# A hybrid decoder layer on one core: new start addresses for the operands of the down products

## The chip, the cores and the metric

The kernel runs on one core of a Trainium2 chip. The metric is the device time of one execution in microseconds (us); smaller is better. TensorE multiplies, VectorE (DVE), ScalarE (ACT) and GpSimd (POOL) do the elementwise work, SyncE (SP) issues most transfers.

## What is computed

One layer over 1056 tokens (1024 of a prompt and 8 x 4 of running sequences), width 1024, all in float32:

```
x = x + 0.5 * rmsnorm(swiglu_ffn(rmsnorm(x, g1), w_gu1, w_down1), p1)      # D_FF = 2816
x = x + rmsnorm(concat(conv_module(u), rg_lru(u)) @ w_out, pm)             # u = rmsnorm(x) @ w_in
x = x + 0.5 * rmsnorm(swiglu_ffn(rmsnorm(x, g2), w_gu2, w_down2), p2)
x = x + rmsnorm(sigmoid(rmsnorm(x) @ w_gate) * (p @ w_proj), pp)

def swiglu_ffn(x, w_gu, w_down):
    gate, up = jnp.split(x @ w_gu, 2, axis=-1)
    return (jax.nn.silu(gate) * up) @ w_down
```

The change concerns `... @ w_down` of both FFNs and `p @ w_proj`, which uses the same buffers.

## The kernel before

**Split products.** Every float32 operand is held as two parts, a high one rounded to the matmul's format (`_hi`) and the rest (`_lo`). A product of two such operands is three TensorE instructions into the same bank of PSUM, always in this order (`passes`, lines 852 to 854): low weights by high activations, high weights by low activations, high by high. Each instruction has its own weight load (PEld in the profile), so the weights that are loaded while the first pass streams are high ones, during the second high ones again, during the third the low ones of the next product.

**Tokens and features.** Features lie on the 128 partitions and tokens along the free dimension. The 1056 tokens are three chunks c = 0, 1, 2 of C = 352 (1408 bytes). `cols(c)` is a chunk's slice.

**An FFN** runs over 11 groups i of 256 hidden features (`NI`), the inner nine in a loop. One group makes, for each chunk, two gate tiles and two up tiles (8 products each over the input features), and then the down products: for each chunk c, for each of eight output tiles m, for the two halves t = 0, 1 of the group, one split product. That is 3 x 4 x 8 x 3 = 288 TensorE instructions and then 3 x 8 x 2 x 3 = 144, each with 128 x 128 weights and 352 columns. `down_products` and `last_downs` issue the latter.

**The elementwise chain** of a group and chunk: VectorE scales gate into `tmp_g` and up into `tmp_u` (line 2212), ScalarE makes silu into `tmp_s` (line 1509), VectorE multiplies it with `tmp_u` into `tmp_a` (line 2223), ScalarE writes `a_hi` (line 1518), VectorE subtracts into `a_lo` (line 2229). Semaphores count each: `silu_done`, `prod_done`, `a_hi_done`, `a_lo_done`. TensorE waits for `a_lo_done` ahead of a chunk's down products. VectorE adds each finished down bank to `acc` (line 2277).

**Addresses.** Buffers are laid out by hand. Every partition has the same layout, so an address is one number of bytes.

```
base = (nc.sbuf_base + 63) // 64 * 64                  # 16512
acc = tile("acc", [P, KT, TOK])                        # at 142592
a_hi = tile("a_hi", [P, G, TOK], F32R)                 # at 176384
a_lo = tile("a_lo", [P, G, TOK], F32R)                 # at 184832
wd_hi, wd_at, _ = place("wd_hi", [P, G * D], F32R)     # at 193280
wd_lo = tile("wd_lo", [P, G * D], F32R)                # at 201472
```

(The addresses behind # follow from the sizes.) `a_hi`, `a_lo`, `wd_hi` and `wd_lo` begin at multiples of 256. A weight tile is 512 bytes, so each starts at a multiple of 256 too. The row of activations for half t and chunk c begins 4224 t + 1408 c bytes on. Modulo 256 both steps are 128, so rows begin at 0 when t + c is even and at 128 when it is odd.

Of the kernel before, what the change touches and what calls it, by code (L numbers as in the profile page):

```python
# [22 lines left out]
F32R = mybir.dt.float32r  # L23
ALU = mybir.AluOpType
ACT = mybir.ActivationFunctionType

P = 128
D = 1024
# [3 lines left out]
PLE = 256  # L32
PT = PLE // P
SEQ, NB, DEC = 1024, 8, 4
TOK = SEQ + NB * DEC
NC = 3
C = TOK // NC
# [6 lines left out]
CG = 8  # L44
CSLOT = BLK // CG
EPS = 1e-6
G = 2
NI = FF // P // G
WIDE = 256
# [3 lines left out]
BANKS = 6  # L53
# [225 lines left out]
def cols(c):  # L279
    return slice(C * c, C * c + C)  # L280


def build(nc, a, out):
    ctx = ExitStack()
    with ctx:

        base = (nc.sbuf_base + 63) // 64 * 64
        at = [base]

        def place(name, shape, dt=F32, offset=None):  # L290
            size = 4
            for s in shape[1:]:
                size *= s
            if offset is None:
                offset = at[0]
                at[0] += (size + 31) // 32 * 32
            t = nc.alloc_sbuf_tensor_at(name, [P] + list(shape[1:]), dt, offset=offset)
            return t, offset, offset + (size + 31) // 32 * 32

        def tile(name, shape, dt=F32):  # L300
            return place(name, shape, dt)[0]

        x_hi = tile("x_hi", [P, KT, TOK], F32R)
        x_lo = tile("x_lo", [P, KT, TOK], F32R)
        wh_at = [at[0], at[0] + 4 * KT * WIDE]
# [5 lines left out]
        rstd_post, norm_at, _ = place("rstd_post", [P, 2, C])  # L311
        ssum = tile("ssum", [P, 2, C])
        std = tile("std", [P, 16])
        sq, sq_at, _ = place("sq", [P, SQ, C])
        ident_r = tile("ident", [P, P], F32R)
        ident = ident_r[:, :].bitcast(F32)
        ones = tile("ones", [P, P])
        params = tile("params", [P, 3 * P])
        half_g = tile("half_g", [P, 2 * KT])
        eps_t = tile("eps_t", [P, 1])  # L320
# [3 lines left out]


        acc = tile("acc", [P, KT, TOK])
        a_hi = tile("a_hi", [P, G, TOK], F32R)
        a_lo = tile("a_lo", [P, G, TOK], F32R)
        wd_hi, wd_at, _ = place("wd_hi", [P, G * D], F32R)
        wd_lo = tile("wd_lo", [P, G * D], F32R)  # L330
        tmp_g, tmp_at, _ = place("tmp_g", [P, 2, C])
        tmp_u = tile("tmp_u", [P, 2, C])
        tmp_s = tile("tmp_s", [P, 2, C])
        tmp_a = tile("tmp_a", [P, 2, C])
        rawd, rawd_at, _ = place("rawd", [P, G * D])
        ffn_end = at[0]

        x_in = place("x_in", [P, 3 * NC - 1, D], offset=pool0)[0]
# [1 line left out]
        rows = place("rows", [P, 3 * P], offset=wd_at)[0]  # L340
        st_rows = place("st_rows", [P, NJ * P], offset=wd_at + 4 * 3 * P)[0]

        p_in = place("p_in", [P, 3 * NC, PLE], offset=tmp_at)[0]
        y_stage, _, e = place("y_stage", [P, 9, D // 2], offset=tmp_at)
        assert e <= ffn_end
        tenth = (WIDE0["ple"] + PLE_SEQ[10][1]) % 2
        y_last = place("y_last", [P, 4, D // 2], offset=wh_at[tenth])[0]
        y_rest = place("y_rest", [P, 2, D // 2], offset=wl_at[tenth])[0]
# [3 lines left out]
        y_hi, yh_at, _ = place("y_hi", [P, KT, TOK], F32R)  # L352
# [4 lines left out]
        gt_last, _, e = place("gt_last", [P, NBLK, BLK], offset=g_at)  # L357
# [3 lines left out]
        gt_even, _, mix_end = place("gt_even", [P, NBLK, BLK], offset=even_at)  # L361
        gt_odd, _, eo = place("gt_odd", [P, NBLK, BLK], offset=yl_at + 6 * row)
        assert eo <= g_at
        assert max(ffn_end, mix_end) <= nc.sbuf_usable_end, (ffn_end, mix_end, nc.sbuf_usable_end)
        zt, _, e = place("zt", [P, SEQ // BLK + NB, BLK], offset=norm_at)
        assert e <= sq_at
        zs, _, e = place("zs", [P, NB, BLK], offset=sq_at)
        lru_a_first, _, e = place("lru_a_first", [P, 2, C], offset=e)
        assert e <= sq_at + 4 * SQ * C
        rev, _, e = place("rev", [P, NJ, 4 * BLK], offset=norm_at)  # L370
# [5 lines left out]
        ux_p, _, e = place("ux_p", [P, 2, LH + C], offset=yh_at)  # L376
        ux_s, _, e = place("ux_s", [P, 2, NB, LH + DEC], offset=e)
# [6 lines left out]
        xc, _, e = place("xc", [P, 2, C], offset=e)  # L384
# [14 lines left out]

        def f32(t):  # L400
            return t.bitcast(F32)

        def lru_a(p):

# [435 lines left out]
        def _(eng):  # L840
# [10 lines left out]
            def passes(dst, wh, wl, xh, xl, first, last):  # L851
                eng.matmul(dst, wl, xh, start=first, stop=False)  # L852
                eng.matmul(dst, wh, xl, start=False, stop=False)  # L853
                return eng.matmul(dst, wh, xh, start=False, stop=last)  # L854
# [70 lines left out]
            def down_products(f, i, c, ms=range(KT), mid=None):  # L925
                Q = NI * NC * G * f
                eng.wait_ge(a_lo_done, i * (NC * G) + (Q + 2 * c + 2))
                for m in ms:
                    off = down_tile(f, i, c, m)
                    bank_at(i * STEP, off)  # L930
                    dst = ps[:, off % BANKS, 0:C]
                    for t in range(G):
                        sl = slice(t * D + m * P, t * D + m * P + P)
                        mm = passes(dst, wd_hi[:, sl], wd_lo[:, sl], a_hi[:, t, cols(c)],
                                    a_lo[:, t, cols(c)], t == 0, t == G - 1)
                    mm.then_inc(psum_full, 1)
                    if mid:
                        mid(m)

            def last_downs(f, mid):  # L940


                i, c = NI - 1, NC - 1
                done = i * (NC * G) + NI * NC * G * f + 2 * c

                def half(m, t):
                    off = down_tile(f, i, c, m)
                    if t == 0:
                        bank_at(i * STEP, off)
                    sl = slice(t * D + m * P, t * D + m * P + P)  # L950
                    mm = passes(ps[:, off % BANKS, 0:C], wd_hi[:, sl], wd_lo[:, sl],
                                a_hi[:, t, cols(c)], a_lo[:, t, cols(c)], t == 0, t == G - 1)
                    if t == G - 1:
                        mm.then_inc(psum_full, 1)

                eng.wait_ge(a_lo_done, done + 1)
                for m in range(AHEAD):
                    half(m, 0)
                eng.wait_ge(a_lo_done, done + 2)
                for m in range(KT):  # L960
                    if m >= AHEAD:
                        half(m, 0)
                    half(m, 1)
                    mid(m)
# [360 lines left out]
            def ple_proj(c, n):  # L1325
                q = n % 4
                for t in range(2):
                    dst = bank(RING["ple", c, q, 2 + t])
                    for k in range(PT):
                        sl = slice(k * D + (2 * q + t) * P, k * D + (2 * q + t) * P + P)  # L1330
                        mm = passes(dst, wd_hi[:, sl], wd_lo[:, sl], a_hi[:, k, cols(c)],
                                    a_lo[:, k, cols(c)], k == 0, k == PT - 1)
                    mm.then_inc(psum_full, 1)

            def ple_unit(s, mid=None):
# [78 lines left out]
        def _(eng):  # L1414
# [96 lines left out]
            def hidden_hi(f, i, c, h):  # L1511

                R, Q = RING["ffn", f], NI * NC * G * f
                eng.wait_ge(prod_done, NC * G * i + (Q + 2 * c + h + 1))

                if not isinstance(i, int) or i:
                    eng.wait_ge(psum_full, STEP * i + (R - STEP + 4 * NC + KT * (c + 1)))
                eng.activation(a_hi[:, h, cols(c)], tmp_a[:, h, :], ACT.Copy).then_inc(a_hi_done, 1)  # L1518

            def hidden_chunk(f, i, c, next_half, hook=None):  # L1520

# [140 lines left out]
            def p_features(c):  # L1662
                for k in range(PT):
                    n = RING["pT", c, k]
                    eng.wait_ge(psum_full, n + 1)
                    eng.activation(a_hi[:, k, cols(c)], ps[:, n % BANKS, 0:C], ACT.Copy
                                   ).then_inc(pt_hi, 1)


# [411 lines left out]
        def _(eng):  # L2081
# [122 lines left out]
            def scaled(f, i, c, h, up):  # L2204

                R, Q = RING["ffn", f], NI * NC * G * f
                q, off = NC * G * i + (Q + 2 * c + h), gate_tile(f, i, c, 2 * up + h)
                src = bank_at(i * STEP, off)
                if f or not isinstance(i, int) or i or c:

                    eng.wait_ge(prod_done if up else silu_done, q - 1)
                eng.tensor_tensor((tmp_u if up else tmp_g)[:, h, :], src, rstd_pre[:, cols(c)],  # L2212
                                  ALU.mult).then_inc(psum_free, 1)

# [11 lines left out]
            def hidden_lo(f, i, c, h):  # L2226
                q = NC * G * i + (NI * NC * G * f + 2 * c + h)
                eng.wait_ge(a_hi_done, q + 1)
                eng.tensor_tensor(a_lo[:, h, cols(c)], tmp_a[:, h, :], f32(a_hi[:, h, cols(c)]),
                                  ALU.subtract).then_inc(a_lo_done, 1)  # L2230

            def hidden_chunk(f, i, c, next_tile, hook=None):
# [148 lines left out]
            def p_features(c):  # L2381
                for k in range(PT):
                    n = RING["pT", c, k]
                    eng.wait_ge(pt_hi, PT * c + k + 1)
                    eng.tensor_tensor(a_lo[:, k, cols(c)], ps[:, n % BANKS, 0:C],
                                      f32(a_hi[:, k, cols(c)]), ALU.subtract
                                      ).then_inc(psum_free, 1)

            def vectors():
# [657 lines left out]
```

## Time and profile before

| | |
|---|---|
| time, median of 3 runs | 2091.97 us (2088.49 to 2093.28) |
| time of the profiled execution | 2089.16 us |
| its span, first to last instruction | 2087.0 us |
| TensorE busy | 2047.6 us, 98% |
| VectorE busy | 1183.3 us, 57% |
| ScalarE busy | 678.8 us, 33% |
| TensorE clock, mean granted | 0.998 of full |

The span is 2.2 us shorter than the execution's own time. A busy share of TensorE counts overlapping instructions once, and a matmul's end is modelled; the distance from one start to the next is what a matmul takes in a stream.

### The profile page before, as it was taken

How to read it: one execution, taken by the hardware profiler on the slowest of the kernel's cores; microseconds unless marked ns; L12 is line 12 of the kernel's file. 1: busy time of each engine (PE TensorE's matmuls, PEld its weight loads, DVE VectorE, ACT ScalarE, POOL GpSimd, SP SyncE). 2: the span in 40 equal slices, each digit the busy share in tenths (PEclk: the TensorE clock that was granted, in tenths of full speed). 3: DMA queues.
4: the chain of work that ended last, by engine and by line, in shares of the span. 5: the costliest groups of instructions: out<-in, count | busy, mean ns of one | idle time of the engine just before them, and what ended most of it. 6: DMA issues, size and time to landing. Idle time of an engine off the chain costs nothing. (4 is left out here: it accounts for less than half of the span.)

```text
span 2087.0 us, 34476 instructions
## 1 busy us (share of the span) xinstructions
PE 2047.6 (98%) x13041; PEld 2032.3 (97%) x13041; DVE 1183.3 (57%) x2367; ACT 678.8 (33%) x1401; POOL 71.6 (3%) x110
## 2 busy tenths in 40 slices
PE   7999999999999999999999999999999999999998
PEld 7999999999999999999999999999999999999997
DVE  5643554354534579547876855345544554368776
ACT  5321222122212234317774532212121212124555
POOL 0000000000000001330000000000000000000000
PEclk9999999999999999999999999999999999999999
DMA  5180111011101101322121211011101111021112
GB/s 168 61 116 26 60 60 43 17 60 60 50 16 55 60 1 51 72 63 45 41 83 61 81 62 61 10 50 60 60 19 41 60 60 38 22 81 42 62 41 104
DMA packets 153277, 116.17 MB, mean 56 GB/s; under 512 B 72648, under 2 KB 143628, under 8 KB 153200
## 3 DMA queue, kind: packets, MB, share of 16 engines
q1 hardware_dynamic: 117728, 108.41, 16.7%
q10 hardware_dynamic: 33424, 5.67, 2.0%
q0 software_dynamic: 2048, 1.06, 0.3%
q8 instruction: 49, 0.80, 0.2%
q14 instruction: 28, 0.23, 0.0%
HBM read 105.96 MB, written 9.15 MB: 55 GB/s over the span
## 5 line engine op out<-in xcount | busy, mean ns | idle before, releaser
L852 PE MATMUL ps<-x_hi,w_lo 128*128 128x352 f32 x2688 | 884.1, 329 | 9.4 <-DVE w_lo L2118 5.1
L854 PE MATMUL ps<-x_hi,w_hi 128*128 128x352 f32 x2688 | 863.7, 321 | 0.0
L853 PE MATMUL ps<-x_lo,w_hi 128*128 128x352 f32 x2688 | 863.7, 321 | 0.0
L852 PEld LDWEIGHTS ps<-x_hi,w_lo 128*128 128x128 f32 x2688 | 506.5, 188 | 12.5 <-issue 6.6
L853 PEld LDWEIGHTS ps<-x_lo,w_hi 128*128 128x128 f32 x2688 | 507.4, 189 | 0.0
L854 PEld LDWEIGHTS ps<-x_hi,w_hi 128*128 128x128 f32 x2688 | 505.2, 188 | 0.0
L852 PE MATMUL ps<-a_hi,wd_lo 128*128 128x352 f32 x1104 | 357.9, 324 | 3.7 <-DVE acc L2916 2.9
L854 PE MATMUL ps<-a_hi,wd_hi 128*128 128x352 f32 x1104 | 354.8, 321 | 0.0
L853 PE MATMUL ps<-a_lo,wd_hi 128*128 128x352 f32 x1104 | 354.6, 321 | 0.0
L2277 DVE TENSOR_TENSOR acc<-ps,acc 128x352 f32<-128x352 f32 x480 | 250.3, 523 | 83.8 <-PE ps L854 77.7
L2212 DVE TENSOR_TENSOR tmp_u<-ps,rstd_pre 128x352 f32<-128x352 f32 x132 | 68.9, 523 | 337.2 <-PE ps L854 337.2
L1439 ACT ACTIVATE w_hi<-raw,params 128x256 fp32r<-128x256 f32 x480 | 200.8, 496 | 120.5 <-DMA raw<-in_ffn_w_gu_dram 109.4
L2118 DVE SCALAR_TENSOR_TENSOR w_lo<-raw,params,w_hi 128x256 fp32r<-128x256 f32 x480 | 212.6, 477 | 24.2 <-ACT w_hi L1439 24.1
L852 PEld LDWEIGHTS ps<-a_hi,wd_lo 128*128 128x128 f32 x1104 | 207.8, 188 | 4.8 <-DVE acc L2916 3.2
L853 PEld LDWEIGHTS ps<-a_lo,wd_hi 128*128 128x128 f32 x1104 | 208.1, 189 | 0.0
L854 PEld LDWEIGHTS ps<-a_hi,wd_hi 128*128 128x128 f32 x1104 | 207.5, 188 | 0.0
L2212 DVE TENSOR_TENSOR tmp_g<-ps,rstd_pre 128x352 f32<-128x352 f32 x132 | 68.5, 522 | 233.2 <-PE ps L854 217.1
L1518 ACT ACTIVATE a_hi<-tmp_a 128x352 fp32r<-128x352 f32 x132 | 60.0, 494 | 406.2 <-DVE tmp_a L2223 406.2
L1509 ACT ACTIVATE tmp_s<-tmp_g 128x352 f32<-128x352 f32 x132 | 65.2, 500 | 383.7 <-DVE tmp_g L2212 383.6
L2142 DVE TENSOR_TENSOR ssum<-ssum,sq 128x352 f32<-128x352 f32 x177 | 92.1, 521 | 12.6 <-ACT sq L1465 5.5
L804 POOL TENSOR_TENSOR std<-std 128x3 f32<-128x3 f32 x27 | 26.4, 976 | 1921.5 <-ACT std L1474 1921.5
L2223 DVE TENSOR_TENSOR tmp_a<-tmp_s,tmp_u 128x352 f32<-128x352 f32 x132 | 62.9, 517 | 14.9 <-ACT tmp_s L1509 14.9
(226 smaller groups left out, 1564.6 us busy)
## 6 DMA issues: line engine op xcount, KB each, us to landing
raw<-in_ffn_w_gu_dram SPq DMA_DIRECT2D x88, 512.0 KB, 3.5
rawd<-in_ffn_w_down_dram SPq DMA_DIRECT2D x22, 1024.0 KB, 7.6
raw<-in_w_in_dram SPq DMA_DIRECT2D x16, 512.0 KB, 4.3
raw<-in_w_out_dram SPq DMA_DIRECT2D x16, 512.0 KB, 3.8
raw<-in_ple_w_gate_dram SPq DMA_DIRECT2D x16, 512.0 KB, 3.7
toeplitz<-rev ACTq DMA_DIRECT2D x8, 512.0 KB, 8.3
x_in<-in_x_prompt_dram SPq DMA_DIRECT2D x4, 512.0 KB, 9.6
toep_first<-toeplitz SPq DMA_DIRECT2D x32, 64.0 KB, 2.3
```

Of the source, the lines that this page charges most:

```text
L804: eng.tensor_tensor(inverse(i), std[:, 8:11], std[:, 12:15], ALU.pow).then_inc(root_done, 1)
L852: eng.matmul(dst, wl, xh, start=first, stop=False)
L853: eng.matmul(dst, wh, xl, start=False, stop=False)
L854: return eng.matmul(dst, wh, xh, start=False, stop=last)
L1439: ins = eng.activation(w_hi[s][:, sl], raw[:, sl], ACT.Copy, scale=vec(gain, k))
L1509: eng.activation(tmp_s[:, h, :], tmp_g[:, h, :], ACT.Silu).then_inc(silu_done, 1)
L1518: eng.activation(a_hi[:, h, cols(c)], tmp_a[:, h, :], ACT.Copy).then_inc(a_hi_done, 1)
L2118: ins = eng.scalar_tensor_tensor(w_lo[s][:, sl], raw[:, sl], vec(gain, k), f32(w_hi[s][:, sl]), ALU.mult, ALU.subtract)
L2142: eng.tensor_tensor(ssum[:, i % 2, :], ssum[:, i % 2, :], sq[:, n % SQ, :], ALU.add).then_inc(add_done, 1)
L2212: eng.tensor_tensor((tmp_u if up else tmp_g)[:, h, :], src, rstd_pre[:, cols(c)], ALU.mult).then_inc(psum_free, 1)
L2223: eng.tensor_tensor(tmp_a[:, h, :], tmp_s[:, h, :], tmp_u[:, h, :], ALU.mult).then_inc(prod_done, 1)
L2277: eng.tensor_tensor(acc[:, m, cols(c)], src, acc[:, m, cols(c)], ALU.add).then_inc(psum_free, 1)
```

## The change

The activations of the down products get a buffer of their own for each chunk, half and part, instead of rows in two large tiles. `tile_at_line` moves the start to the next address that is 64 x `line` bytes behind a multiple of 256. Rows of chunk 0 begin at 0, of chunk 1 at 128 and of chunk 2 at 64, for both halves and both parts. `wd_hi` begins at 64, `wd_lo` at 0 (modulo 256). To make room for the gaps, `tmp_a` shares the buffer of `tmp_u`, `ones` keeps the 2 columns that are read, and `rawd` moves ahead of `tmp_g`. VectorE's scaling of an up tile now waits for `a_lo_done` where it waited for `prod_done`.

```diff
+LINE = 64
+A_LINES = ((0, 0), (2, 2), (1, 1))
+WD_LINES = (0, 1)
...
+        def tile_at_line(name, shape, line, dt=F32R):
+
+            at[0] += (4 * LINE + line * LINE - at[0]) % (4 * LINE)
+            return place(name, shape, dt)
+
...
-        ones = tile("ones", [P, P])
+        ones = tile("ones", [P, 2])
...
-        a_hi = tile("a_hi", [P, G, TOK], F32R)
-        a_lo = tile("a_lo", [P, G, TOK], F32R)
-        wd_hi, wd_at, _ = place("wd_hi", [P, G * D], F32R)
-        wd_lo = tile("wd_lo", [P, G * D], F32R)
+        act = {(c, t, part): tile_at_line(f"a_{part}{c}{t}", [P, C], A_LINES[c][part == "lo"])[0]
+               for c in range(NC) for part in ("hi", "lo") for t in range(G)}
+        wd_hi, wd_at, _ = tile_at_line("wd_hi", [P, G * D], WD_LINES[1])
+        wd_lo = tile_at_line("wd_lo", [P, G * D], WD_LINES[0])[0]
+        rawd, rawd_at, _ = place("rawd", [P, G * D])
         tmp_g, tmp_at, _ = place("tmp_g", [P, 2, C])
         tmp_u = tile("tmp_u", [P, 2, C])
         tmp_s = tile("tmp_s", [P, 2, C])
-        tmp_a = tile("tmp_a", [P, 2, C])
-        rawd, rawd_at, _ = place("rawd", [P, G * D])
+        tmp_a = tmp_u
...
-                        mm = passes(dst, wd_hi[:, sl], wd_lo[:, sl], a_hi[:, t, cols(c)],
-                                    a_lo[:, t, cols(c)], t == 0, t == G - 1)
+                        mm = passes(dst, wd_hi[:, sl], wd_lo[:, sl], a_hi(c, t),
+                                    a_lo(c, t), t == 0, t == G - 1)
...
-                    eng.wait_ge(prod_done if up else silu_done, q - 1)
+                    eng.wait_ge(a_lo_done if up else silu_done, q - 1)
```

The program's order stays as it was. On TensorE the first output tile of the first down products of chunk 0 reads as follows, before (a name's last number is the buffer's, `_69` is `a_hi`, `_70` is `a_lo`):

```order
L852 MATMUL ps<-a_hi_69,wd_lo_72 128x352 [waits psum_free,a_lo_done,down_lo]
L853 MATMUL ps<-a_lo_70,wd_hi_71 128x352
L854 MATMUL ps<-a_hi_69,wd_hi_71 128x352
L852 MATMUL ps<-a_hi_69,wd_lo_72 128x352
L853 MATMUL ps<-a_lo_70,wd_hi_71 128x352
L854 MATMUL ps<-a_hi_69,wd_hi_71 128x352
```

and of the change, where a name ends in chunk and half:

```order
L868 MATMUL ps<-a_hi00_69,wd_lo_82 128x352 [waits psum_free,a_lo_done,down_lo]
L869 MATMUL ps<-a_lo00_71,wd_hi_81 128x352
L870 MATMUL ps<-a_hi00_69,wd_hi_81 128x352
L868 MATMUL ps<-a_hi01_70,wd_lo_82 128x352
L869 MATMUL ps<-a_lo01_72,wd_hi_81 128x352
L870 MATMUL ps<-a_hi01_70,wd_hi_81 128x352
```

The same six instructions with the same waits; the second three now read a buffer of their own instead of the second row of `a_hi` and `a_lo`.

On VectorE, at the end of the first chunk's hidden features, before:

```order
L2223 TENSOR_TENSOR tmp_a_76<-tmp_s_75,tmp_u_74 128x352 [waits psum_free,silu_done] x2
L2229 TENSOR_TENSOR a_lo_70<-tmp_a_76,a_hi_69 128x352 [waits a_hi_done] x2
L2212 TENSOR_TENSOR tmp_g_73<-ps,rstd_pre_56 128x352 [waits silu_done,psum_full,spread_out]
L2212 TENSOR_TENSOR tmp_g_73<-ps,rstd_pre_56 128x352 [waits silu_done,psum_full]
...
L2212 TENSOR_TENSOR tmp_u_74<-ps,rstd_pre_56 128x352 [waits prod_done,psum_full]
```

and of the change:

```order
L2239 TENSOR_TENSOR tmp_u_85<-tmp_s_86,tmp_u_85 128x352 [waits psum_free,silu_done] x2
L2245 TENSOR_TENSOR a_lo00_71<-tmp_u_85,a_hi00_69 128x352 [waits a_hi_done]
L2245 TENSOR_TENSOR a_lo01_72<-tmp_u_85,a_hi01_70 128x352 [waits a_hi_done]
L2228 TENSOR_TENSOR tmp_g_84<-ps,rstd_pre_56 128x352 [waits silu_done,psum_full,spread_out]
L2228 TENSOR_TENSOR tmp_g_84<-ps,rstd_pre_56 128x352 [waits silu_done,psum_full]
...
L2228 TENSOR_TENSOR tmp_u_85<-ps,rstd_pre_56 128x352 [waits a_lo_done,psum_full]
```

Here the product is written over `tmp_u`, and the next up tile waits for the subtraction, which VectorE has issued itself some rows earlier.

## Rows read from the trace of the kernel before

**Rows 1.** The page: TensorE's busy time, share and instructions; granted clock in 40 slices.

```profile
PE 2047.6 (98%) x13041; PEld 2032.3 (97%) x13041; DVE 1183.3 (57%) x2367; ACT 678.8 (33%) x1401; POOL 71.6 (3%) x110
...
PEclk9999999999999999999999999999999999999999
```

**Rows 2.** What TensorE waited for: total us, times, longest.

```profile
PE ps L1041 <- DMA x_in<-in_x_prompt_dram: 7.7, 1, 7.7
PE ps L852 <- DVE w_lo L2118: 5.1, 3, 2.1
```

**Rows 3.** Busy time by stretches: three chunks' down products, then a whole pass.

```profile
213.13:220.76 7.63, 7.63 (x50) 7.63 (x49) 7.08 (x16) 4.13 (x10) 0.00 (x0) 1.00 0.20 64
220.76:228.39 7.63, 7.63 (x50) 7.63 (x49) 6.69 (x15) 1.71 (x4) 0.00 (x0) 1.00 0.72 251
228.39:236.02 7.63, 7.63 (x50) 7.63 (x49) 4.84 (x10) 0.00 (x0) 0.00 (x0) 1.00 0.30 92
...
213.13:281.79 68.66, 68.66 (x434) 68.66 (x433) 32.34 (x65) 15.29 (x30) 0.00 (x0) 1.00 0.14 46
```

**Rows 4.** Down products in the groups by line: busy us, mean ns.

```profile
L852 PE MATMUL ps<-a_hi,wd_lo 128*128 128x352 f32 x1104 | 357.9, 324 | 3.7 <-DVE acc L2916 2.9
L854 PE MATMUL ps<-a_hi,wd_hi 128*128 128x352 f32 x1104 | 354.8, 321 | 0.0
L853 PE MATMUL ps<-a_lo,wd_hi 128*128 128x352 f32 x1104 | 354.6, 321 | 0.0
```

**Rows 5.** Timeline of TensorE, chunk 0: start us, us; the first tile, and the last's end.

```profile
77.72 0.32 PE L852 MATMUL ps<-a_hi,wd_lo 128*128 128x352 f32 x1
77.88 0.32 PE L853 MATMUL ps<-a_lo,wd_hi 128*128 128x352 f32 x1
78.05 0.32 PE L854 MATMUL ps<-a_hi,wd_hi 128*128 128x352 f32 x1
78.20 0.32 PE L852 MATMUL ps<-a_hi,wd_lo 128*128 128x352 f32 x1
78.36 0.32 PE L853 MATMUL ps<-a_lo,wd_hi 128*128 128x352 f32 x1
78.52 0.32 PE L854 MATMUL ps<-a_hi,wd_hi 128*128 128x352 f32 x1
78.67 0.32 PE L852 MATMUL ps<-a_hi,wd_lo 128*128 128x352 f32 x1
...
1834.83 0.32 PE L852 MATMUL ps<-a_hi,wd_lo 128*128 128x352 f32 x1
```

**Rows 6.** Timeline of TensorE where chunk 0 gives way to chunk 1.

```profile
288.95 0.32 PE L852 MATMUL ps<-a_hi,wd_lo 128*128 128x352 f32 x1
...
289.90 0.33 PE L852 MATMUL ps<-a_hi,wd_lo 128*128 128x352 f32 x1
```

**Rows 7.** Timeline of TensorE where chunk 1 gives way to chunk 2.

```profile
296.58 0.32 PE L852 MATMUL ps<-a_hi,wd_lo 128*128 128x352 f32 x1
...
297.53 0.32 PE L852 MATMUL ps<-a_hi,wd_lo 128*128 128x352 f32 x1
```

**Rows 8.** Timelines of weight loads and of products, start of a down stage.

```profile
281.80 0.19 PEld L853 LDWEIGHTS ps<-a_lo,wd_hi 128*128 128x128 f32 x1
...
281.79 0.32 PE L852 MATMUL ps<-a_hi,wd_lo 128*128 128x352 f32 x1
```

**Rows 9.** Timeline of VectorE, chunk 0 of a pass, into chunk 1.

```profile
251.92 0.95 DVE L2223 TENSOR_TENSOR tmp_a<-tmp_s,tmp_u 128x352 f32<-128x352 f32 x2
253.08 0.96 DVE L2229 TENSOR_TENSOR a_lo<-tmp_a,a_hi 128x352 fp32r<-128x352 f32 x2 [0.21 <-ACT a_hi L1518]
...
262.92 0.53 DVE L2212 TENSOR_TENSOR tmp_u<-ps,rstd_pre 128x352 f32<-128x352 f32 x1 [3.29 <-PE ps L854]
```

More of the change, by code:

```diff
@@ L341, in build @@
         st_rows = place("st_rows", [P, NJ * P], offset=wd_at + 4 * 3 * P)[0]
-        p_in = place("p_in", [P, 3 * NC, PLE], offset=tmp_at)[0]
-        y_stage, _, e = place("y_stage", [P, 9, D // 2], offset=tmp_at)
-        assert e <= ffn_end
+        p_in, _, e = place("p_in", [P, 3 * NC, PLE], offset=tmp_at)
+        assert e <= nc.sbuf_usable_end
+        y_stage, _, e = place("y_stage", [P, 9, D // 2], offset=rawd_at)
+        assert e <= nc.sbuf_usable_end
         tenth = (WIDE0["ple"] + PLE_SEQ[10][1]) % 2
@@ L401, in f32, with a_hi, a_lo @@
             return t.bitcast(F32)
+        def a_hi(c, t):
+            return act[c, t, "hi"][:, :]
+        def a_lo(c, t):
+            return act[c, t, "lo"][:, :]
         def lru_a(p):
@@ L951, in half @@
                     mm = passes(ps[:, off % BANKS, 0:C], wd_hi[:, sl], wd_lo[:, sl],
-                                a_hi[:, t, cols(c)], a_lo[:, t, cols(c)], t == 0, t == G - 1)
+                                a_hi(c, t), a_lo(c, t), t == 0, t == G - 1)
                     if t == G - 1:
@@ L1330, in ple_proj @@
                         sl = slice(k * D + (2 * q + t) * P, k * D + (2 * q + t) * P + P)
-                        mm = passes(dst, wd_hi[:, sl], wd_lo[:, sl], a_hi[:, k, cols(c)],
-                                    a_lo[:, k, cols(c)], k == 0, k == PT - 1)
+                        mm = passes(dst, wd_hi[:, sl], wd_lo[:, sl], a_hi(c, k),
+                                    a_lo(c, k), k == 0, k == PT - 1)
                     mm.then_inc(psum_full, 1)
@@ L1517, in hidden_hi @@
                     eng.wait_ge(psum_full, STEP * i + (R - STEP + 4 * NC + KT * (c + 1)))
-                eng.activation(a_hi[:, h, cols(c)], tmp_a[:, h, :], ACT.Copy).then_inc(a_hi_done, 1)
+                eng.activation(a_hi(c, h), tmp_a[:, h, :], ACT.Copy).then_inc(a_hi_done, 1)
             def hidden_chunk(f, i, c, next_half, hook=None):
@@ L1665, in p_features @@
                     eng.wait_ge(psum_full, n + 1)
-                    eng.activation(a_hi[:, k, cols(c)], ps[:, n % BANKS, 0:C], ACT.Copy
+                    eng.activation(a_hi(c, k), ps[:, n % BANKS, 0:C], ACT.Copy
                                    ).then_inc(pt_hi, 1)
@@ L2228, in hidden_lo @@
                 eng.wait_ge(a_hi_done, q + 1)
-                eng.tensor_tensor(a_lo[:, h, cols(c)], tmp_a[:, h, :], f32(a_hi[:, h, cols(c)]),
+                eng.tensor_tensor(a_lo(c, h), tmp_a[:, h, :], f32(a_hi(c, h)),
                                   ALU.subtract).then_inc(a_lo_done, 1)
@@ L2384, in p_features @@
                     eng.wait_ge(pt_hi, PT * c + k + 1)
-                    eng.tensor_tensor(a_lo[:, k, cols(c)], ps[:, n % BANKS, 0:C],
-                                      f32(a_hi[:, k, cols(c)]), ALU.subtract
+                    eng.tensor_tensor(a_lo(c, k), ps[:, n % BANKS, 0:C],
+                                      f32(a_hi(c, k)), ALU.subtract
                                       ).then_inc(psum_free, 1)
```

## The prediction

> **What bounds the kernel now.** I read the page first. TensorE is busy for 98% of a span of 2087.0 us, at a granted clock of 0.9 or more in every slice, so at its level of 2.4 GHz [rows 1]. The list of what TensorE waited for holds little: its longest entry is 7.7 us for the first input, once [rows 2]. So the time is a sum over TensorE's instructions, and the question is how far apart they start. A table by stretches says it for the inside of the FFN loops: one pass of the loop takes 68.66 us, and VectorE is busy for 32.34 us of it, ScalarE for 15.29 [rows 3]. A pass has 432 products of 352 columns (288 of gate and up, 144 of down), so they start 158.9 ns apart. At 2.4 GHz 352 columns are 146.7 ns. What lies between, 12.2 ns a product, is the only stock from which a change of addresses can draw, and in the down products alone.
>
> How many these are: 1104 in each of the three passes, 3312 in all [rows 4]. 0.2% of the time is 4.2 us, about what a measurement of this kernel can tell from no change. Spread over 3312 products that is 1.27 ns each.
>
> **Do addresses matter at all?** The timeline of TensorE answers this. The six products of one output tile start at 77.72, 77.88, 78.05, 78.20, 78.36, 78.52 and the next tile at 78.67 [rows 5]. The rows are printed to 0.01 us; over 95 such tiles (five in the first chunk of each of 19 down stages, the first and last of them in [rows 5]) the trace's own times average to distances of 160.9, 161.6, 155.8, 160.9, 154.9 and 159.2 ns, with a scatter of 0.6 to 0.8 ns. Instruction, shape and clock are the same in all six. What differs is the row of activations: the first three read `a_hi` or `a_lo` for t = 0, whose start is a multiple of 256 bytes; the last three read t = 1, 4224 bytes on, which is 128 bytes behind one. In chunk 1 it is the other way round, and the two triples (478.3 and 475.1 ns) change places with it.
>
> There are two places in a pass where six products in a row read at one alignment, since t = 1 of the last tile of a chunk and t = 0 of the next chunk agree. From chunk 0 to 1 all six are at 128 bytes: 288.95 to 289.90, over 19 such places 949.3 ns [rows 6], 158.2 each. From chunk 1 to 2 all six are at 0: 296.58 to 297.53, over 19 places 958.5 ns [rows 7], 159.75 each. The normal mixture is 953.4, 158.9 each. All weights stand at 0 in these. So relative alignment is worth 1.5 ns a product between its two values that this kernel has, with single distances between 154.9 and 161.9 ns.
>
> Which two reads are it? The weights of the next product are loaded while the present one streams: the load for `a_lo,wd_hi` begins at 281.80, the product before it at 281.79 [rows 8]. So I describe a product by d, the start of the weights that are loaded during it less the start of the rows that it streams, modulo 256. Before, d is 0 for three products and 128 for three.
>
> The Trainium skill speaks against all of this. Its page "TensorE: Matmul & The Clock Gate", Part 2, gives TensorE two independent read ports and says: "Loading the next tile's weights doesn't steal SBUF read bandwidth from the running matmul"; the page "SBUF — State Buffer", section "Who interferes with whom", adds that TensorE waits for nobody. By that rule no address changes anything and the sum is 0. The trace disagrees in size, not by much: 949.3 against 958.5 ns for the same instructions. The first page's distance between products, columns over clock and 2.5 ns more, would make 149.2 here, an estimate from that page, against 158.9 measured; if five places in nine came down to that, it would be worth some 18 us.
>
> **The change part by part.** *Alignment.* Every chunk's rows stand at one offset now, both t and both parts. High weights are at 64, low ones at 0. The first and second pass of a product load high weights for the next, the third loads low ones. So d becomes 64, 64, 0 in chunk 0 (rows at 0), 192, 192, 128 in chunk 1 (rows at 128), and 0, 0, 192 in chunk 2 (rows at 64). Of nine places three have d = 0, one has 128, and five (two at 64, three at 192) have a value that no product of 352 columns shows in this trace. The four known ones cost 3 x 159.75 + 158.2 = 637.45 ns against 4 x 158.9 = 635.6 before: 1.85 ns more. For the five unknown ones the nearest rows are the shortest and the longest single distance between products, 154.9 and 161.9. I take their middle, 158.4, since the two alignments that are known fall on either side of it by about a nanosecond and nothing in the rows says on which side 64 bytes lie: 5 x (158.4 - 158.9) = -2.5 ns. Together -0.65 ns over nine products, and over 3312 (368 nines) -0.2 us.
> The ends: at 154.9 the five give -20 + 1.85 = -18.15 ns, times 368 -6.7 us. At 161.9 they give 15 + 1.85 = 16.85 ns, +6.2 us. The far end is the clock itself, 146.7 ns: 5 x -12.2 + 1.85 = -59.2, -21.8 us.
>
> *tmp_a becomes tmp_u.* The product of silu and up is written over up. VectorE's scaling of the next up tile then waits for `a_lo` of the chunk before, not for the product. Behind the wait on VectorE stand the product of that chunk and the sums of the down banks, for which TensorE would wait in the end. But VectorE issues that `a_lo` itself, ahead of the scaling: it ends at 253.08 + 0.96 = 254.04, and the next up tile is scaled at 262.92, because TensorE has only then made it [rows 9]. The cover is 8.9 us, and without it a scaling would be late by one subtraction, 0.5 us. The product's in-place write has the same shape as before. I cost it at nothing.
>
> *The rest.* `ones` shrinks to the two columns that are read; buffers behind it, `params` among them, move; `acc`, `tmp_g` and `y_stage` keep their offset modulo 256. No instruction, transfer or order changes. For VectorE and ScalarE a new row start could cost something on 132 conversions and subtractions of 0.5 us; both engines have half of each pass to spare [rows 3]. Nothing.
>
> The sum is -0.2 us on the profiled execution's 2089.2 us. The median of the runs shown, 2092.0, lies 2.8 us above that execution, and the same step from it gives 2091.7.
>
> **The rivals.** *A: 64 bytes apart the two reads miss each other, and it is faster.* For it: alignment is visible, and the best single distance, 154.9, occurs at d = 128, so part of the 12.2 ns is a collision that can be avoided. Against it: at a constant d = 128 the six still average 158.2, since 155 is followed by 159 and 161; a saving at one product is largely paid at the next. At 154.9 in all five places the time is 2092.0 - 6.7 = 2085.3. It counts as faster from a mean of 158.9 - (11.4 + 1.85)/5 = 156.2 ns in the five places (11.4 ns in nine products being 4.2 us). Its far tail, down to 2070, needs products at the bare clock.
>
> *B: 64 or 192 is the worse place, and it is slower.* The mechanism: high and low weights no longer start alike, so rows that suit one load do not suit the other, and the 159 and 161 ns distances come at each pass. In the five places 161.9 gives 2092.0 + 6.2 = 2098.2. It decides from a mean of 158.9 + (11.4 - 1.85)/5 = 160.8. For it: longest distances are the more frequent ones already (four of six are 159 or more). Against it: no alignment known has a mean above 159.75.
>
> *C: nothing happens*, because only 128 bytes count, and 64 is half way between. Then the five places average 158.9 and the time is 2092.7. It shares its outcome with the forecast.
>
> **How the numbers follow.** The forecast with C gets 0.43: the known means lie within 0.9 ns of the mixture, and the five unknown would have to leave 156.2 to 160.8. A gets 0.35, since its tail is long and the stock of 12.2 ns is real; B gets 0.22. The predicted time is 2091.7. The range reaches past A's and B's times to 2081 and 2099; what is left out is A's far tail and a little of B. The chances of faster, same and slower are 0.35, 0.43 and 0.22. For the forecast alone the range is 2088 to 2096.
>
> **What would show it.** In the profile after, the gate and up products stay at 288 in 45.77 us of a pass. The 48 down products of a chunk took 7.63 us in each chunk [rows 3]; they now differ by chunk. By my terms chunk 2, with two places in three at d = 0, has about 7.65; chunk 0 and 1 carry the unknown: chunk 0 at 154.9 in its two unknown places would show 16 x (2 x 154.9 + 159.75) ns = 7.51 us, at 161.9 7.74. A pass has 16 nines of down products, so 68.66 - 16 x 0.018 = 68.37 us is A and 68.93 is B. VectorE waiting for itself ahead of `tmp_u` would show the reuse to cost. The prediction is wrong if an alignment of 64 bytes has a mean outside 156.2 to 160.8, or if the distances depend on something else than d, such as the address of the rows alone or the step from one product's rows to the next's.

## The result, and the profile after

The changed kernel takes 2097.59 us (median of 18 runs, 2095.74 to 2110.43) against 2091.45 us for the kernel before in the same rounds (18 runs). The ratio is 1.0031, with a 95% interval of 1.0016 to 1.0046: slower by 0.3%. Four of the change's 18 executions (2108.0 to 2110.4 us, at a mean granted clock of 0.990 to 0.991 where the others had 0.997 or 0.998) and five of the kernel before (2101.1 to 2104.6 us) are some 12 us longer, and the medians of the others, 2097.1 and 2090.6 us, have the same ratio. The forecast was no measurable change at 2091.7 us with a range of 2081 to 2099 us; the time lies in the range and where rival B had put it (2098.2 us), which had the smallest chance.

The page of the profiled execution (2095.96 us) has the same shape as before. Its span is 6.8 us longer, and TensorE is busy for 7.1 us more:

```profile
span 2093.8 us, 34476 instructions
PE 2054.7 (98%) x13041; PEld 2039.9 (97%) x13041; DVE 1183.8 (57%) x2367; ACT 679.2 (32%) x1401; POOL 71.9 (3%) x110
PEclk9999999999999999999999999999999999999999
L868 PE MATMUL ps<-a_hi,wd_lo 128*128 128x352 f32 x1104 | 357.2, 324 | 3.6 <-DVE acc L2932 2.9
L870 PE MATMUL ps<-a_hi,wd_hi 128*128 128x352 f32 x1104 | 358.1, 324 | 0.0
L869 PE MATMUL ps<-a_lo,wd_hi 128*128 128x352 f32 x1104 | 357.3, 324 | 0.0
```

Set beside [rows 1] and [rows 4], the last three rows show where it went but not how: a matmul's recorded duration covers the overlap with its neighbour, so the busy time rises by 6.0 us in two lines (3.3 and 2.7) and falls by 0.7 in the third. The distance between starts is what counts. TensorE's timeline at the edges of one pass of the FFN loop (start us, duration us) gives it: first gate product, first down product of chunks 0, 1 and 2, first gate product of the next pass.

```profile
168.53 0.32 PE L868 MATMUL ps<-x_hi,w_lo 128*128 128x352 f32 x1
...
214.30 0.32 PE L868 MATMUL ps<-a_hi,wd_lo 128*128 128x352 f32 x1
...
221.98 0.32 PE L868 MATMUL ps<-a_hi,wd_lo 128*128 128x352 f32 x1
...
229.76 0.32 PE L868 MATMUL ps<-a_hi,wd_lo 128*128 128x352 f32 x1
...
237.48 0.32 PE L868 MATMUL ps<-x_hi,w_lo 128*128 128x352 f32 x1
```

The gate and up products take 45.77 us as before. The down products of a chunk take 7.68, 7.79 and 7.72 us where each took 7.63 [rows 3]. A pass is 68.95 us instead of 68.66, 0.293 us more by the trace's own times; there are 3312/144 = 23 passes' worth of down products, so 6.7 us, the whole difference of the spans.

Inside chunk 1 a tile of six products now starts like this:

```profile
223.44 0.32 PE L868 MATMUL ps<-a_hi,wd_lo 128*128 128x352 f32 x1
223.60 0.32 PE L869 MATMUL ps<-a_lo,wd_hi 128*128 128x352 f32 x1
223.76 0.33 PE L870 MATMUL ps<-a_hi,wd_hi 128*128 128x352 f32 x1
223.92 0.32 PE L868 MATMUL ps<-a_hi,wd_lo 128*128 128x352 f32 x1
224.09 0.32 PE L869 MATMUL ps<-a_lo,wd_hi 128*128 128x352 f32 x1
224.25 0.33 PE L870 MATMUL ps<-a_hi,wd_hi 128*128 128x352 f32 x1
224.41 0.32 PE L868 MATMUL ps<-a_hi,wd_lo 128*128 128x352 f32 x1
```

Six products take 0.97 us here and 0.95 in [rows 5]. Over 95 tiles the distances average 160.9, 161.7, 164.1 and again the same three ns in chunk 1 (973.3 for six), 157.5, 160.9, 161.6 in chunk 0 (960.0), and 967.1 for six in chunk 2, whose first tiles are shorter (its 7.72 us are 965 for six). Before it was 953.4 everywhere. (The 95 tiles are five of a chunk's eight, in 19 down stages.)

The wait that came with the shared buffer is free. The chain on VectorE has the same gaps as in [rows 9]: `a_lo` ends at 254.54 + 0.96 = 255.50 and the next up tile is scaled at 264.38, on TensorE's word.

```profile
253.38 0.95 DVE L2239 TENSOR_TENSOR tmp_u<-tmp_s,tmp_u 128x352 f32<-128x352 f32 x2
254.54 0.96 DVE L2245 TENSOR_TENSOR a_lo<-tmp_u,a_hi 128x352 fp32r<-128x352 f32 x2 [0.21 <-ACT a_hi L1534]
...
264.38 0.52 DVE L2228 TENSOR_TENSOR tmp_u<-ps,rstd_pre 128x352 f32<-128x352 f32 x1 [3.29 <-PE ps L870]
```

### The profile page after: what moved, and what is told of

Same layout as the page of the kernel before. It is cut to its first block and busy times, and to the rows that moved or that the text cites. A ratio compares the mean times of both kernels' runs of the same rounds, so it can differ in the third digit from the quotient of the medians.

```text
span 2093.8 us, 34476 instructions
## 1 busy us (share of the span) xinstructions
PE 2054.7 (98%) x13041; PEld 2039.9 (97%) x13041; DVE 1183.8 (57%) x2367; ACT 679.2 (32%) x1401; POOL 71.9 (3%) x110
## 5 line engine op out<-in xcount | busy, mean ns | idle before, releaser
L1534 ACT ACTIVATE a_hi<-tmp_u 128x352 fp32r<-128x352 f32 x132 | 60.0, 494 | 406.2 <-DVE tmp_u L2239 406.2
L2239 DVE TENSOR_TENSOR tmp_u<-tmp_s,tmp_u 128x352 f32<-128x352 f32 x132 | 62.9, 517 | 14.9 <-ACT tmp_s L1525 14.9
```

The source lines that it names most:

```text
L1534: eng.activation(a_hi(c, h), tmp_a[:, h, :], ACT.Copy).then_inc(a_hi_done, 1)
L2239: eng.tensor_tensor(tmp_a[:, h, :], tmp_s[:, h, :], tmp_u[:, h, :], ALU.mult).then_inc(prod_done, 1)
```

## The experiments

All start from the changed kernel. `WD_LINES` gives low and high weights, in steps of 64 bytes (modulo 256); where `a_line(c, t, lo)` appears, it replaces the table `A_LINES`. In all of them `rawd` is kept behind the mixer's `y_lo` (`at[0] = max(at[0], pool0 + 8 * KT * TOK)`), which by the sizes moves anything only in e3, and there only buffers that no product reads. I read every run by the distances inside the loops, since the passes of a loop agree within some 2 ns, where a single execution's time doesn't tell 2 us. The single executions took, in order of number from e5 to e8, 2103.99, 2106.13, 2095.12 and 2098.36 us, e2 2102.03, and e10 to e14 and e16 2096.88, 2098.50, 2093.61, 2097.34, 2096.66 and 2101.35.

### First round: the two parts of the change, its frame, and a chain of rows

**e1_weights_alike**: the rows of the change, weights alike.

```diff
-WD_LINES = (0, 1)
+WD_LINES = (0, 0)
```

> Part of the change alone: rows of the three chunks at 0, 128 and 64 bytes as in the change, but high weights at 0 like the low ones. Theory D (a product costs by d, the start of the weights loaded during it less the start of its rows): chunk 0 has d = 0 throughout, 48 x 159.75 = 7.67 us; chunk 1 d = 128, 48 x 158.2 = 7.59 us; chunk 2 d = 192, about 7.74 us by what the changed kernel shows for 192. Theory S (step: what costs is that the next product's rows no longer begin where the last ones ended, modulo 256, which once in three products was so before): all three chunks alike, 7.68 us or more. Theory W (high and low weights starting at different offsets costs): all chunks at 7.63 us as before.

TensorE's timeline at the starts of the three chunks and of the next gate products:

```profile
213.15 0.32 PE L869 MATMUL ps<-a_hi,wd_lo 128*128 128x352 f32 x1
...
220.83 0.32 PE L869 MATMUL ps<-a_hi,wd_lo 128*128 128x352 f32 x1
...
228.43 0.32 PE L869 MATMUL ps<-a_hi,wd_lo 128*128 128x352 f32 x1
...
236.10 0.32 PE L869 MATMUL ps<-x_hi,w_lo 128*128 128x352 f32 x1
```

7.68, 7.60 and 7.68 us; one run of 2089.66 us. Chunks 0 and 1 fall within 0.01 us of where theory D has them (160.0 and 158.3 ns a product), chunk 2 0.06 us lower than D had it. Theory S (7.68 us or more in all) fails at chunk 1, and theory W (7.63 us in all) at each. The down products of a pass are 0.066 us over before, where the change has 0.293: rows at one offset are worth little, and most of the change's cost needs the high weights at 64.

**e2_rows_alternate**: the weights of the change, rows as before.

```diff
+def a_line(c, t, lo):
+    return 2 * ((t + c) % 2)
```

> The other part alone: high weights at 64 and low ones at 0 as in the change, rows alternating between 0 and 128 bytes by half and chunk as before. Theory D, with the changed kernel's means of 159.2 ns for d = 64 and 161.2 for d = 192: 48 x 159.8 = 7.67 us a chunk. Theory S: 7.63 us as before. Theory W: 7.70 us or more in each chunk.

Measured 7.77, 7.78 and 7.79 us, 972 to 973 ns for six products in each chunk. The unlike weights cost 20 ns for six with the old rows, more than D's 7.67; of the three theories only W had 7.70 or more, and W had failed in e1. And something that no theory had: the gate and up products, whose instructions, operands and addresses are untouched, take 45.87 us a pass instead of 45.77. The first four of their twelve tiles are slower (3.84 us instead of 3.81), the other eight are as before.

**e3_layout_only**: separate buffers, shared `tmp_u`, the new wait, but rows as in e2 and weights alike. 

> The change without any change of alignment: buffers for each chunk and half, tmp_a in tmp_u, the wait for a_lo_done, rawd ahead of tmp_g, but rows alternating 0 and 128 and both weights at 0, as before. Theories D, S and W all say 7.63 us a chunk, 68.66 us a pass and a ratio to the kernel before of 1.000. If the reuse of tmp_u cost anything, the ratio would be above 1.001 and VectorE would show waits ahead of tmp_u.

Measured 7.63, 7.63 and 7.63 us, a ratio of 1.0012 with an interval of 0.9989 to 1.0035. The frame of the change costs nothing. It is the trace that says so: a pass takes 68.66 us as before, while the interval of the ratio would still hold the change's 1.0031.

**e4_rows_follow_on**: weights alike, `a_line` returns `2 * ((t + c + lo) % 2)`. 

> Both weights at 0; high and low activations at opposite offsets (0 and 128), alternating by half, so that in every step from product to product the next rows begin where the last ones ended modulo 256. Theory D: the mixture of d = 0 and 128 as before, 7.63 us a chunk, ratio 1.000. Theory S: the distances of 155 to 159 ns that stand at such a step before come at every product, 7.44 to 7.55 us a chunk, 2 to 5 us in all per 2 ns saved: a ratio of 0.994 to 0.997. Theory W: 7.63.

Measured 7.76, 7.77 and 7.75 us and a ratio of 1.0041 (1.0027 to 1.0056). Theory S, that rows which follow on are cheap, is refuted: it is slower with that at every step. D and W fail too (they had 7.63).

### Second round: does anything additive in the offsets explain it?

Four kernels with one execution each. **e5_weights_64_alike**: `WD_LINES = (1, 1)`, rows `(0, 3, 1)[c]`. **e6_weights_128_apart**: `WD_LINES = (0, 2)`, rows of the change. **e7_low_weights_64**: `WD_LINES = (1, 0)`, rows of the change. **e8_rows_apart**: `WD_LINES = (0, 0)`, rows `((0, 1), (0, 2), (2, 0))[c][lo]`.

> Both weights at 64, rows of the three chunks at 0, 192 and 64 bytes, so d is 64, 128 and 0 and constant in each chunk. It fills in d = 64 and tests whether only the difference counts. Theory D (the distances of a product add up by d): 160.0 ns a product in chunk 2 (7.68 us a chunk), 158.3 in chunk 1 (7.60), as the run with both weights at 0 gave; chunk 0 must then be 160.0 to explain the changed kernel's chunk 0 (480.0 ns a triple at d = 64, 64, 0). Theory U (what costs is that the starts within one split product are unlike, in weights or in rows, whatever d they give): all three chunks between 7.59 and 7.69. If the address itself counted and not the difference, chunks 1 and 2 would leave 7.60 and 7.68.

> High weights at 128, low weights at 0, rows of the chunks at 0, 128 and 64 bytes: the change with twice the distance between the weights. Theory D, with 160.0 for d of 0 and 192 and 158.3 for 128: chunk 0 (d = 128, 128, 0) 16 x 476.7 ns = 7.63 us, chunk 1 (0, 0, 128) 7.65. Theory U: every chunk above 7.68, by as much as or more than in the changed kernel (7.68, 7.79 and 7.72).

> Weights the other way round: low at 64, high at 0, rows of the chunks at 0, 128 and 64 bytes. Theory D: chunk 0 (d = 0, 0, 64) 7.68 us, chunk 1 (128, 128, 192) 7.63, chunk 2 (192, 192, 0) 7.68. Theory U: slower than with weights alike (7.68, 7.60, 7.68) in most or all chunks, with a mean over the chunks of 7.70 or more, since the starts are again unlike.

> Both weights at 0; only the rows of high and low activations begin at different offsets, the same for both halves: 0 and 64 in chunk 0, 0 and 128 in chunk 1, 128 and 0 in chunk 2. Theory D: chunk 0 (d = 0, 192, 0) 7.68 us, chunk 1 (0, 128, 0) 7.65, chunk 2 (128, 0, 128) 7.63. Theory U: all three above 7.70, as where rows alternated at every product (7.76).

Chunks and gate products of a pass, in us:

| run | high, low weights | rows of the chunks | chunk 0 | 1 | 2 | gate, up |
|---|---|---|---|---|---|---|
| before | 0, 0 | 0 and 128 in turn | 7.63 | 7.63 | 7.63 | 45.77 |
| the change | 64, 0 | 0, 128, 64 | 7.68 | 7.79 | 7.72 | 45.77 |
| e5 | 64, 64 | 0, 192, 64 | 7.68 | 7.98 | 7.72 | 45.87 |
| e6 | 128, 0 | 0, 128, 64 | 7.72 | 7.64 | 7.71 | 46.32 |
| e7 | 0, 64 | 0, 128, 64 | 7.68 | 7.69 | 7.68 | 45.87 |
| e8 | 0, 0 | 0/64, 0/128, 128/0 | 7.78 | 7.68 | 7.78 | 45.77 |

Theory U fails: e7's weights are as unlike as the change's, and its chunks average 7.68, where U wanted 7.70 or more; e6's chunk 1 (7.64) and e8's (7.68) lie below what U had; and e5 has everything alike and its chunk 1 is the slowest of all. D fails by that chunk: d = 128 gave 158.3 ns in e1 and gives 166.7 here. The last column fails every theory in which a product's cost follows from its own addresses.

### Third round: memory

By now theory M stood: the two streams of TensorE, rows and weights, fall into one of several rhythms, and the offsets only decide which rhythms there are; which one is taken depends on how TensorE comes in.

**e9_all_128**: `WD_LINES = (0, 0)`, all rows at 128. 

> The best pair seen so far everywhere: both weights at 0, every row at 128. If a chunk's rate follows from its own offsets: 158.3 ns a product, 7.60 us in all three chunks, 0.09 us a pass and 2 us in all less than before, a ratio of 0.999, which five rounds may or may not tell from 1. If a chunk's rate depends on the rhythm in which TensorE enters it (theory M, memory), chunks 0 and 2 may differ from 7.60, and the gate products behind them may leave their 45.77 us a pass.

Measured 7.60 us in all three chunks (950 ns for six) and a ratio of 0.9993 (0.9979 to 1.0008). The two intervals (this one and 1.0016 to 1.0046) don't meet, so it is faster than the change; by its time it can't be told from the kernel before, and by the trace it has 0.09 us a pass less. It is the best of what was run. The chunks are what their own offsets say, so M isn't needed here.

```profile
230.87 0.32 PE L872 MATMUL ps<-a_hi,wd_lo 128*128 128x352 f32 x1
...
238.47 0.32 PE L872 MATMUL ps<-x_hi,w_lo 128*128 128x352 f32 x1
```

These are the edges of chunk 2, for comparison with e11.

**e10_chunks_permuted**: `WD_LINES = (0, 2)`, rows `(1, 0, 2)[c]`. 

> High weights at 128, low ones at 0 as in the earlier run with weights 128 apart, where rows at 0, 128 and 64 gave 7.72, 7.64 and 7.71 us and the unchanged gate products took 46.32 us a pass instead of 45.77. Only the order of the rows is changed, to 64, 0 and 128. Theory M (a rhythm, once entered, is kept on into the next products): the gate products leave 46.32, and the chunks' times need not be the same for the same rows. Without memory: chunks 7.71, 7.72, 7.64 and gate products at one value for all kernels.

The gate products are back at 45.77 us, with a change in the down rows alone. The chunks themselves keep their rates with their rows: 7.72, 7.74 and 7.65.

**e11_rows_192**: `WD_LINES = (0, 0)`, rows `(3, 1, 2)[c]`. 

> Both weights at 0, rows of the chunks at 192, 64 and 128. With both weights at 64, rows at 192 took 166.7 ns a product. If rows at 192 are slow by themselves (they touch seven blocks of 256 bytes where the others touch six), chunk 0 takes 7.8 to 8.0 us. If only the difference d counts, chunk 0 has d = 64, which gave 7.68. Chunks 1 and 2 as with the same rows before: 7.68 and 7.60, unless the rhythm at entry counts.

The edges of a pass, as above:

```profile
215.26 0.33 PE L872 MATMUL ps<-a_hi,wd_lo 128*128 128x352 f32 x1
...
222.95 0.32 PE L872 MATMUL ps<-a_hi,wd_lo 128*128 128x352 f32 x1
...
230.64 0.33 PE L872 MATMUL ps<-a_hi,wd_lo 128*128 128x352 f32 x1
...
238.63 0.32 PE L872 MATMUL ps<-x_hi,w_lo 128*128 128x352 f32 x1
```

Rows at 192 are not slow (7.69). But chunk 2 has rows at 128 and weights at 0, the very pair of e1's chunk 1 and of all of e9, and takes 7.99 us, 1000 ns for six products instead of 950. For e9 the match goes further than modulo 256: by the sizes, chunk 2's rows (from 188288) and both weights (194304 and 202496) lie at the same addresses in both kernels, so no rule on single addresses, whatever its modulus, tells them apart. Nor does the work beside it: in these 48 products VectorE is busy for 4.83 us in e11 and 4.84 in e9, ScalarE for none, and the DMA share is 0.30 in both. What differs is the offset of the rows that TensorE read just before, 64 here and 128 in e9.

**e12_64_rows_192_last**: `WD_LINES = (1, 1)`, rows `(1, 0, 3)[c]`. 

> Both weights at 64 as in the run that gave 7.68, 7.98 and 7.72 us for rows at 0, 192 and 64; now rows at 64, 0 and 192. If the rate follows from the offsets: 7.72 or 7.68, 7.68 and 7.98 us. Theory M: chunk 2 is not at 7.98, or chunk 0 is at 7.68 where it was 7.72, and the gate products of a pass, 45.87 us in that run, move.

7.68, 7.69 and 7.61 us: rows at 192 with weights at 64 took 7.98 in the middle of e5 and take 7.61 at the end here. Here the rows lie at other addresses than in e5. The gate products are back at 45.76 us a pass, from e5's 45.87. All three are what M had: not even the full pair of offsets decides.

### Fourth round: the same addresses, another entry

**e14_rows_192_extra**: e11 with one small product more, whose result the next one replaces.

```diff
                     dst = ps[:, off % BANKS, 0:C]
+                    if c == 2 and m == 0:
+                        eng.matmul(ps[:, off % BANKS, 0:P], wd_lo[:, 0:P], a_hi(c, 0)[:, 0:P],
+                                   start=True, stop=True)
```

> The kernel with both weights at 0 and rows at 192, 64 and 128, whose chunk 2 took 7.99 us (1000 ns for six products) although rows at 128 gave 7.60 (950 ns) in three other runs; and one product of 128 columns more in front of chunk 2's 48, into a bank that the next product starts anew. No address changes. Theory M: the extra product shifts the rhythm, the 48 products may run at 950 ns for six, and the pass is shorter for more work. Theory O: 1000 ns for six stays, and the pass is 0.11 us or so longer.

The extra product and the first of chunk 2, a tile in the middle of it, and the next gate product:

```profile
230.57 0.22 PE L953 MATMUL ps<-a_hi,wd_lo 128*128 128x128 f32 x1
230.63 0.38 PE L872 MATMUL ps<-a_hi,wd_lo 128*128 128x352 f32 x1
...
234.01 0.32 PE L872 MATMUL ps<-a_hi,wd_lo 128*128 128x352 f32 x1
...
234.96 0.32 PE L872 MATMUL ps<-a_hi,wd_lo 128*128 128x352 f32 x1
...
238.28 0.32 PE L872 MATMUL ps<-x_hi,w_lo 128*128 128x352 f32 x1
```

A tile is back at 0.95 us. (Rows at 128 with weights at 0 had given 950 ns in two runs, e1 and e9, not three; e12's 950 ns are for rows at 192 and weights at 64.) The extra product takes 0.06 us, chunk 2's own 48 take 7.65, and the pass is 0.28 us shorter than in e11, for more work at the same addresses. This shows the memory without any change of layout: what went ahead of the 48 products sets their rate.

**e15_change_extra**: the changed kernel itself with the same small product ahead of chunk 1 (`c == 1`). 

> The changed kernel with one product of 128 columns more in front of chunk 1's 48, as above. Chunk 1 had 973.3 ns for six products. Theory M: it may leave 973.3 in either direction. If it stays at 973.3, then high weights at 64 and low ones at 0 have no better rhythm with rows at 128 that this shift reaches, and the cost of the change is one of its offsets (theory O).

```profile
217.08 0.32 PE L869 MATMUL ps<-a_hi,wd_lo 128*128 128x352 f32 x1
...
224.75 0.22 PE L950 MATMUL ps<-a_hi,wd_lo 128*128 128x128 f32 x1
224.81 0.38 PE L869 MATMUL ps<-a_hi,wd_lo 128*128 128x352 f32 x1
...
232.55 0.32 PE L869 MATMUL ps<-a_hi,wd_lo 128*128 128x352 f32 x1
...
240.23 0.33 PE L869 MATMUL ps<-x_hi,w_lo 128*128 128x352 f32 x1
```

Chunk 1 goes from 973.3 to 960.0 ns for six (7.74 us), chunk 2 with it from 967 to 960 (7.68). The pass of down products is 23.15 us with the extra 0.06 in it, 0.03 less than the change has without it. The execution's total, 2110.5 us, says nothing on this: its clock was low for 27 us outside the loops (below).

**e13_change_permuted**: the change with rows `(1, 0, 2)[c]`. 

> The change with the rows of its chunks in another order: 64, 0 and 128 instead of 0, 128 and 64; weights as in the change (high 64, low 0). Theory O (a chunk's rate follows from its own offsets): 7.72, 7.68 and 7.79 us, 23.18 us of down products a pass as in the changed kernel. Theory M (the rhythm at entry counts, offsets only set which rhythms exist): at least one chunk differs from that by 0.03 us or more, and the sum leaves 23.18.

7.73, 7.68 and 7.79 us, 23.20 against 23.18: within 0.013 us of what theory O had for each chunk. In this run M, as I had put it (0.03 us or more for one chunk), is wrong: the change's rates came with its rows. So entry can matter and often doesn't; rows at 128 with high weights at 64 took 973 ns for six in both orders and 960 only when pushed.

**e16_apart_gate_extra**: e6 with a product of 128 columns of x by `w_lo` ahead of a pass's first gate tile. 

> The kernel with weights 128 apart, whose unchanged gate and up products took 46.32 us a pass instead of 45.77, with one product of 128 columns more in front of a pass's first gate tile. Theory M: gate and up products leave 46.32 and may fall to about 45.77 + 0.11 = 45.9 us. Theory O has no reason for 46.32 at all, and says that it stays, plus 0.11.

```profile
168.90 0.23 PE L994 MATMUL ps<-x_hi,w_lo 128*128 128x128 f32 x1
...
214.89 0.32 PE L869 MATMUL ps<-a_hi,wd_lo 128*128 128x352 f32 x1
```

Gate and up products with the extra one take 45.985 us, 0.34 less than without it in e6. Tile by tile, the first four take 3.84 us (the very first 3.89) and the other eight 3.81, the rate of the kernel before.

e6 itself shows the same without an edit. TensorE enters the first pass of the second FFN's loop after a pause, 0.44 us from start to start, where it enters the others 0.16 us behind the last down product. The addresses are those of every other pass. That pass's gate and up products take 45.87 us, the others 46.32; one tile of an ordinary pass and the same tile of that one:

```profile
242.87 0.32 PE L869 MATMUL ps<-x_hi,w_lo 128*128 128x352 f32 x1
...
246.74 0.32 PE L869 MATMUL ps<-x_hi,w_lo 128*128 128x352 f32 x1
...
1247.95 0.32 PE L869 MATMUL ps<-x_hi,w_lo 128*128 128x352 f32 x1
...
1251.77 0.32 PE L869 MATMUL ps<-x_hi,w_lo 128*128 128x352 f32 x1
```

3.87 and 3.82 us for the same 24 products.

## Why the prediction was wrong

*What bounds the kernel* was right: a sum of distances between TensorE's starts and nothing else. The span grew by what the down products grew, 6.7 of 6.8 us.

*"The rest" and the shared `tmp_u`* were right: 0 predicted, and e3 has 7.63 us a chunk and 68.66 us a pass.

*That addresses matter* was right. The rule of the Trainium skill, page "TensorE: Matmul & The Clock Gate", Part 2, that a weight load does not take read bandwidth from the running matmul, was taken in the prediction to make the sum 0. Measured is a ratio of 1.0031, and 158.3 to 166.7 ns a product over all runs; here the measurement decides that addresses count. That it is the weight load that takes the time is not shown by any run.

*The step that failed* is "So I describe a product by d", and with it the sum over nine places. It took the four places with d = 0 or 128 as known, at 637.45 ns together. In the changed kernel they take 161.6, 164.1, 161.3 and 161.4, 648.4 ns. These known places are 11 ns over their term. The five unknown ones average 160.4 instead of 158.4, 10 ns over theirs, and alone would still have been inside the 156.2 to 160.8 that the text gave for "same". (These are interior tiles; over whole chunks nine products take 1448.9 ns, where the sum had 1429.5.) Both signs of being wrong that the prediction named came: places with d = 192 average 161.2 ns, above 160.8, and one d has several values (d = 128: 158.2 before, 164.1 now). Rival B, slower at 2098.2 us, hit the time, in part by luck: it put nearly all of its 6.2 us on the five unknown places (15 of 16.85 ns in nine products), and more than half of the measured rise lies in the four known ones (12.8 of some 20 ns). Its reason, that rows which suit one load don't suit the other, is not shown; its own sentence "no alignment known has a mean above 159.75" was the same mistake, since 159.75 and 158.2 were means of one rhythm.

What stands in its place: the distance follows from the whole arrangement and from what went before, not from d. e2 isolates the weights' part: 20 ns more for six with the rows left alone. e1 isolates the rows' part: 0.066 us a pass. That the weights are unlike is not the reason by itself: e7's are unlike too and its down products take 0.16 us a pass more than before, e5's are alike and take 0.50 more. Together they aren't additive (0.44 and 0.07 us a pass alone, 0.29 both). And the addresses of a product don't fix its distance: chunk 2 of e9 and e11 has the same ones and takes 7.60 and 7.99 us, and e14 and e15 move the rate with no address changed.

There was a sign of it in the trace of before. Where chunk 0 gives way to chunk 1, the last three of six products at one alignment had other distances than the first three (157.4, 161.9, 154.9 after 160.8, 155.2, 159.1). I averaged them instead of asking why the same three instructions differ.

What stays open: why a rhythm is 950, 960, 973 or 1000 ns for six products, and why the change's own chunk 1 falls into the one of 973. That two streams, rows and weights, fall into step is my picture of it; the runs show only that the rate depends on what went before. No run here takes the two readers apart, and a cause such as banks of the memory was not tested. Whether the kernel can be brought into a rhythm below 158.3 ns a product is open too.

## What to carry to other kernels

In a kernel that is bound by a dense stream of matmuls, read the distance between starts, by position in the inner pattern, over many repetitions: in this kernel the passes of a loop agree within 2 ns in 68.66 us, where a ratio of times had an interval of some three thousandths. Start addresses of rows and weights move it by up to 5% (158.3 to 166.7 ns here), but not by a rule that can be added up product by product, so a layout has to be measured in place, in its final order. Of the layouts run here, all weights at one offset and all rows of all chunks 128 bytes from it (e9) was the fastest, 158.3 ns in every chunk. It is the layout as a whole that was: the same pair in a single chunk behind rows at other offsets took 166.7 ns (e11's chunk 2, e5's chunk 1).

## What the hardware showed that I had not expected

**Rhythms that survive their cause.** Gate and up products, untouched, took 45.77, 45.87 or 46.32 us a pass depending on the layout of the down products ahead of them. A slower rate held for the first four tiles of a pass, those of chunk 0 (3.84 us a tile in e2, e5 and e7, instead of 3.81), or in e6 for all twelve (3.87 us in eight and 3.84 in four), and it changed only where a chunk ended. Most chunks run at 950, 953.3, 960, 966.7, 973.3 or 1000 ns for six products, with a scatter of under 1 ns; others lie between (970 in e4, 964 in e6 and e10), some with a scatter of 2 to 6 ns.

**More work, less time.** One product of 128 columns made a pass 0.28 us shorter (e14).

**A fall of the clock outside the loops.** In the profiled executions of e15 and e4, and not in the changed kernel's, TensorE's granted clock shows a slice below 9 in the mixer stage, where products of 48 columns stand between the wide ones:

```profile
PEclk9999999999999999999799999999999999999999
```

For 27 us it was at 1.2 GHz (a granted clock of 0.50), and e15's execution took 2110.5 us, although its passes were shorter than the changed kernel's. TensorE had been busy for 26.8 of the 29.3 us before the fall. In the changed kernel's execution it was busy for 25.5 of 28.0 us in the same stage and the clock stayed at 1.00, so what decides it is open.
